# Reordering a split-precision input projection: high-part products two tiles ahead, the last chunks' splits earlier, the decode rows' transposes one block later

## The chip, the cores and the metric

The kernel runs on one NeuronCore of one Trainium2 chip. The metric is device time in microseconds from the start to the end of the program. Besides the plain timed runs there is one profiled execution; its trace gives the start and end of every instruction on the five engines: TensorE (PE; its weight loads are PEld), VectorE (DVE), ScalarE (ACT), GpSimd (POOL) and SyncE (SP), which here issues nearly all DMA copies (SPq is its queue).

## The reference

One inference step of a hybrid decoder layer for two request groups: a prompt of 512 tokens and 8 decode rows of one token each, model width 1024, float32.

```python
def mix_input(x, pos, g_norm_mix, w_in, g_q, g_k):
    xn = rms_norm(x, g_norm_mix)
    z = xn @ w_in                                  # (1024 x 3072)
    q, k, v, b_gate, c_gate, u_in = jnp.split(z, SPLITS, axis=-1)   # 768,768,768,256,256,256
    q = rope(rms_norm(heads(q), g_q), pos)
    k = rope(rms_norm(heads(k), g_k), pos)
    return q, k, heads(v), b_gate, c_gate * u_in
# attention: 12 heads x 64, dilated causal windows (128,1), (512,4), (2048,16), merged by their denominators;
#   the decode rows read a cache of 1024 earlier keys and values
# short convolution over c_gate * u_in, gated by b_gate; both parts normed, then w_out (1024 x 1024)
# h = x + mix;  y = h + HierMoE(rms_norm(h)): 32 experts of width 256, two per token
```

The outputs are y for both groups, the keys and values of the prompt and of the decode rows, and the convolution's last rows.

## The kernel before

The program has stages that follow one another: norm and transpose of x; the input projection (to about 222 us); attention of the prompt by 24 pairs of heads; output projection and routing; 16 pairs of experts, whose weights are streamed; the sum of the results. The change lies in the input projection.

**Split precision.** w_in is loaded in 8 chunks of 384 columns (`wchunk`). Each chunk is split into a rounded copy `w_high` (ScalarE, `high(c, i)`, four pieces of a chunk) and the rest `w_low` = w - w_high (VectorE, `low(c, i)`, four pieces, written over the loaded chunk). x has been split in the same way into `xT_high` and `xT_low`. A product then has three parts: x_high by w_high and x_low by w_high (16 matmuls, here called the high part) and x_high by w_low (8 matmuls, the low part).

**Chunks 0 to 5** (q, k, v) are computed token tile by token tile (4 tiles, `t`), a tile of a chunk being a unit `n = 4c + t` that accumulates in bank `n % 3`: high part (L671, L672), low part (L676). Between units TensorE does small work for the 8 decode rows: `partial_sums(c+1)` (L652, the decode rows times the unsplit next chunk, before `low` overwrites it), `combine(c)` (L603, adds its four parts), and `turn_rot` (L593, transposes of a rotated q or k tile, three units behind; it waits until ScalarE has copied the transposes before out of bank 5, L1043).

**VectorE's norm and rotation**, `norm_rope`, runs once for each q or k unit and once for a chunk's decode rows: a sum of squares (L1302), then, after a root on ScalarE (L1049), a reciprocal (L1304), products (L1225), half of them on GpSimd (L1763), and a sum. The pieces `low(c+1, i)` of the next chunk are done between these. All of L1225 is one helper, `tt`.

**Decode scores.** `sample_scores(b)` on VectorE, b = 0 to 7, multiplies 1 row of q, copied to all partitions (`spread_q`, a DMA issued by SyncE), by the cached keys, and sums by head (L1225, L1327). SyncE issues key, q, value and chunk copies in one fixed order, and each waits for a score step or a chunk to be done. The scores are transposed by TensorE (`turn_scores`, L616, L618), VectorE and ScalarE form the softmax, `turn_probs` (L626, L628) transposes the probabilities, VectorE places them, and `sample_values(0)` and `sample_values(1)` (L640) multiply them by the cached value rows of sequences 0 to 3 and 4 to 7. The second four use the buffers of the first: SyncE loads them once `sample_values(0)` is done (`v_used`).

**Chunks 6 and 7** (B, C, u) are computed as 6 blocks `i` of 128 columns by all 512 tokens, high part L724 and L725, low part L729, with the decode steps in between. After the 6 blocks come `sample_values(1)`, `own_values` and the pairs of heads. SyncE loads w_out when block 5 is done, behind the last value rows in its queue.

Each engine works through its own list in order; semaphores join them.

Of the kernel before, what the change touches and what calls it, by code (L numbers as in the profile page):

```python
# [26 lines left out]
P = 128  # L27
SEQ, DEC, D = 512, 8, 1024
NT = SEQ // P
# [91 lines left out]
def build(nc, x_prompt, x_sample, cache_k, cache_v, state_conv, g_norm_mix, w_in, g_q, g_k, w_conv, g_attn_out,  # L121
# [3 lines left out]
    with ctx:  # L125
# [436 lines left out]
        def _(pe):  # L562
# [92 lines left out]

            partial_sums(0)
            pend = []
            for c in range(QKV_CHUNKS):
                pe.wait_ge(S["w_high_done"], 4 * (c + 1))
                for t in range(NT):  # L660
                    n = unit(c, t)

                    if 3 <= n < QK_CHUNKS * NT + 3:
                        pe.wait_ge(S["z_copied"], n - 2)
                    elif n >= 3:
                        pe.wait_ge(S["v_evac"], n - 2 - QK_CHUNKS * NT)
                    cols = slice(t * P, (t + 1) * P)
                    if c == 0:
                        pe.wait_ge(S["x_evac"] if t < 2 else S["x_evac_p"], 2 * (t % 2) + 2)
                    for k in range(KD):  # L670
                        pe.matmul(bank[n % 3][:, 0:CW], xT_high[:, k, cols], w_high[c][:, k, :], start=(k == 0), stop=False)  # L671
                        pe.matmul(bank[n % 3][:, 0:CW], xT_low[:, k, cols], w_high[c][:, k, :], start=False, stop=False)  # L672
                    if t == 0:
                        pe.wait_ge(S["w_low_done"], 4 * (c + 1))
                    for k in range(KD):
                        last = pe.matmul(bank[n % 3][:, 0:CW], xT_high[:, k, cols], w_low[c][:, k, :],  # L676
                                         start=False, stop=(k == KD - 1))
                    last.then_inc(S["z_done"], 1)
                    if (c, t) == (0, 0):
                        turn_state()  # L680
                    if t == 0 and c <= 4 or (c, t) == (5, 2):
                        partial_sums(c + 1)
                    if t == 1:
                        combine(c)
                    if c < QK_CHUNKS:
                        pend.append((c, t))
                    if len(pend) > 3 or (c >= QK_CHUNKS and pend):
                        turn_rot(*pend.pop(0))
# [25 lines left out]
            for i in range(6):  # L714
# [16 lines left out]
                if i == 0:  # L731
                    combine(6)
                    turn_scores()
# [1161 lines left out]
```

## Time and profile before

| | us |
|---|---|
| median of 3 runs (674.38, 675.0, 678.39) | 675.0 |
| the profiled execution's own time | 671.45 |
| its span, first to last instruction | 669.8 |
| TensorE busy in the span | 545.2 (81%) |
| VectorE busy | 286.7 (43%) |
| ScalarE busy | 149.5 (22%) |
| GpSimd busy | 104.3 (16%) |

The mean granted clock of TensorE is 0.92 of 2.4 GHz. The page's slices show two stretches in which the DMA engines are almost wholly busy, in the experts' stage, and the input projection as a stretch in which TensorE and VectorE are both busy. A share of busy time is a mean over stages, so the rows below are taken from the projection alone. Times in the timelines are us from the start of the span; a row gives start, length, engine, line, operation, output and inputs, partitions and shape, the count, and in brackets the idle time of the engine before it with what ended it.

### The profile page before, as it was taken

Reading aid. Unit: us, or ns where it says so; the run is one execution under the profiler, and the core shown is the slowest. Engines: PE = TensorE matmul, PEld = TensorE weight load, DVE = VectorE, ACT = ScalarE, POOL = GpSimd, SP = SyncE. Lnnn points to the kernel's source line nnn. Section 1 sums busy time; section 2 is a strip of 40 time slices with the busy share of each in tenths; the row PEclk is TensorE's granted clock in tenths of the full one; section 3 lists DMA queues with packets and bytes.
Section 4 is the critical chain, followed back from the end, with each engine's and each line's share of the span. In section 5 each row is a group of like instructions: output and inputs, shape, how many; then the busy total and the mean of one; then the engine's idle time right before and its main releaser. Section 6 shows DMA issues by size and latency. Waiting matters only on the chain.

```text
span 669.8 us, 7971 instructions
## 1 busy us (share of the span) xinstructions
PE 545.2 (81%) x2798; PEld 323.0 (48%) x2798; DVE 286.7 (43%) x647; ACT 149.5 (22%) x351; POOL 104.3 (16%) x141
## 2 busy tenths in 40 slices
PE   3698889898599999899999516899996869797930
PEld 3486788797376588763555412333332323233300
DVE  4866776876521578732467440211211111111107
ACT  5433343323121356730000100210110000000000
POOL 0333454400000000000002232112212110201000
PEclk9998999999699999979999756999999898989975
DMA  7942323177906900029601901899999999999819
GB/s 267 292 129 93 97 72 139 35 248 243 304 0 187 375 7 1 1 83 426 279 31 54 386 1 55 365 421 420 420 420 420 421 420 421 420 422 419 335 50 353
DMA packets 42931, 159.66 MB, mean 238 GB/s; under 512 B 9048, under 2 KB 18208, under 8 KB 30584
## 3 DMA queue, kind: packets, MB, share of 16 engines
q1 hardware_dynamic: 36816, 146.95, 57.1%
q0 software_dynamic: 6080, 12.26, 4.9%
q8 instruction: 20, 0.33, 0.2%
q14 instruction: 15, 0.12, 0.1%
HBM read 151.56 MB, written 16.05 MB: 250 GB/s over the span
## 4 chain that ended last, share of the span: by engine, by line
PE 38%; SPq 21%; DVE 14%; DMA 10%; issue 8%; ACT 5%; POOL 3%; POOLq 0%; DVEq 0%; ACTq 0%
SPq L486 11%; PE bank L935 6%; SPq L500 6%; PE bank L890 4%; PE bank L960 4%; PE bank L791 3%; SPq L495 3%; DMA x<-q_rows 3%; POOL ring L1763 3%; DMA ring<-in_w_down_dram 3%; DVE work L1225 2%; PE bank L702 2%; PE bank L776 2%; DVE split L1225 2%; PE bank L676 2%
## 5 line engine op out<-in xcount | busy, mean ns | idle before, releaser
L935 PE MATMUL bank<-ring,work 128*64 128x512 f32 x512 | 121.7, 631 | 21.8 <-DMA ring<-in_w_up_dram 20.4
L935 PEld LDWEIGHTS bank<-ring,work 128*64 128x64 f32 x512 | 39.8, 145 | 102.1 <-issue 84.7
L671 PE MATMUL bank<-split 128*128 128x384 f32 x192 | 66.8, 348 | 0.0
L960 PE MATMUL bank<-ring,work 128*64 128x512 f32 x256 | 60.2, 613 | 7.6 <-ACT work L1198 7.6
L1225 DVE TENSOR_TENSOR work<-work,bank 128x256 f32<-128x256 f32 x16 | 6.7, 421 | 138.4 <-ACT work L1194 138.4
L672 PE MATMUL bank<-split 128*128 128x384 f32 x192 | 64.7, 337 | 0.0
L1763 POOL TENSOR_TENSOR ring<-ring 128x192 f32<-128x192 f32 (+1 forms) x40 | 38.0, 967 | 48.9 <-DVEq L1313 48.9
L890 PE MATMUL bank<-ring 128*128 128x512 f32 x96 | 42.6, 595 | 0.0
L676 PE MATMUL bank<-split 128*128 128x384 f32 x192 | 38.2, 340 | 4.5 <-DVE split L1225 4.5
L1225 DVE TENSOR_TENSOR split<-ring,split 128x768 fp32r<-128x768 f32 (+1 forms) x36 | 39.8, 1144 | 2.0 <-PE bank L652 1.6
L671 PEld LDWEIGHTS bank<-split 128*128 128x128 f32 x192 | 36.4, 190 | 3.8 <-issue 1.3
L1793 POOL DMA_DIRECT2D hn_rows<-work x5 | 2.8, 564 | 223.4 <-DVE work L1589 223.4
L960 PEld LDWEIGHTS bank<-ring,work 128*64 128x64 f32 x256 | 17.3, 139 | 40.1 <-issue 28.7
L676 PEld LDWEIGHTS bank<-split 128*128 128x128 f32 x192 | 33.6, 189 | 6.1 <-DVE split L1225 6.1
L672 PEld LDWEIGHTS bank<-split 128*128 128x128 f32 x192 | 36.5, 190 | 0.0
L1147 ACT ACTIVATE ring<-ring,st 128x512 f32<-128x512 f32 (+3 forms) x48 | 26.6, 554 | 42.5 <-DVE st L1397 42.5
L1667 DVE COPY work<-bank 128x512 f32<-128x512 f32 x16 | 11.1, 692 | 57.8 <-PE bank L960 57.8
L1194 ACT ACTIVATE work<-bank 128x256 f32<-128x256 f32 x16 | 6.1, 384 | 122.7 <-PE bank L935 122.6
L1225 DVE TENSOR_TENSOR work<-bank,gain_f 128x512 f32<-128x512 f32 (+1 forms) x42 | 26.0, 660 | 16.0 <-issue 14.0
L944 PE MATMUL bank<-ident,work 128*128 128x128 f32 x128 | 18.4, 289 | 16.6 <-DMA work<-hn_rows,pay_sb 16.6
L791 PE MATMUL bank<-ring 128*128 128x64 f32 x240 | 29.9, 271 | 0.4 <-DVE ring L1225 0.3
L791 PEld LDWEIGHTS bank<-ring 128*128 128x128 f32 x240 | 28.7, 192 | 0.9 <-DVE ring L1225 0.8
(214 smaller groups left out, 762.3 us busy)
## 6 DMA issues: line engine op xcount, KB each, us to landing
ring<-in_w_down_dram SPq DMA_DIRECT2D x32, 1024.0 KB, 27.3
ring<-in_w_gate_dram SPq DMA_DIRECT2D x30, 1024.0 KB, 19.8
ring<-in_w_up_dram SPq DMA_DIRECT2D x30, 1024.0 KB, 22.8
ring<-in_w_in_dram SPq DMA_DIRECT2D x8, 1536.0 KB, 9.6
x<-in_x_prompt_dram SPq DMA_DIRECT2D x8, 512.0 KB, 7.9
ring<-in_w_out_dram SPq DMA_DIRECT2D x1, 4096.0 KB, 13.1
ring<-results SPq DMA_DIRECT2D x4, 1024.0 KB, 7.8
x<-q_rows SPq DMA_DIRECT2D x8, 384.0 KB, 6.4
```

Of the source, the lines that this page charges most:

```text
L486: sp.dma_start(gate_up[s][h][:, o, :, :], w[0, ds(e, 1)].rearrange("e (p k) f -> p (e k) f", p=P)).then_inc(gu_in[s], 16)
L500: sp.dma_start(down[s][h], w_down[0, ds(e, 1)].rearrange("e (p k) n -> p (e k) n", p=P)).then_inc(dn_in[s], 16)
L671: pe.matmul(bank[n % 3][:, 0:CW], xT_high[:, k, cols], w_high[c][:, k, :], start=(k == 0), stop=False)
L672: pe.matmul(bank[n % 3][:, 0:CW], xT_low[:, k, cols], w_high[c][:, k, :], start=False, stop=False)
L676: last = pe.matmul(bank[n % 3][:, 0:CW], xT_high[:, k, cols], w_low[c][:, k, :], start=False, stop=(k == KD - 1))
L791: last = pe.matmul(bank[6 + u % 2][:, h * DH:(h + 1) * DH], probs_t[u % 2][h][:, j * P:(j + 1) * P], v_rows[:, j, (2 * hp + h) * DH:(2 * h ...
L890: last = pe.matmul(bank[g][:, :], src, wout[:, k, cols], start=(k == rng[0]), stop=(k == rng[-1]))
L935: last = pe.matmul(bank[2][64 * h:64 * h + 64, :], xgT[:, k, 64 * h:64 * h + 64], gate_up[s][h][:, :, k, :], start=(k == 0), stop=(k == KD ...
L960: last = pe.matmul(bank[4 + j][64 * h:64 * h + 64, :], hT[:, c, 64 * h:64 * h + 64], down[s][h][:, c, j * 512:(j + 1) * 512], start=(c == ...
L1147: act.activation(buf, buf, ACT.Exp, bias=nmax[:, u % 4:u % 4 + 1], scale=-1.0, accum_out=den[:, u % 24:u % 24 + 1]).then_inc(S["exp_done"], 1)
L1225: return dve.tensor_tensor(out, a, b, op)
L1763: last = pool.tensor_tensor(sv[:, :, a * half:(a + 1) * half], zv[:, :, b * half:(b + 1) * half], bc(rope_g[2 * (cc // 2) + 1][0:w, t, a * ...
```

## The change

In chunks 0 to 5 the high parts of tiles 0 and 1 are computed one after the other, then the low part of tile 0, and, behind the small work that stood there, the low part of tile 1. Tiles 2 and 3 are as before. The wait for `w_low` stands before the first low part.

Chunk 6's split moves: on ScalarE two high pieces behind unit (5, 1) and two behind (5, 2), instead of one each behind (5, 1) and (5, 2), and two behind (5, 3); on VectorE two low pieces each behind `sample_scores(5)` and `sample_scores(6)`, instead of three behind `sample_scores(7)` and one behind the decode rows' own scores. Chunk 7's low pieces move ahead of the placing of the probabilities; its high pieces ahead of the softmax's exponential on ScalarE.

On TensorE `turn_scores` moves from behind block 0 to behind block 1, `turn_probs` from block 1 to block 2, and `sample_values(0)` from block 3 to block 4.

```diff
             for c in range(QKV_CHUNKS):
                 pe.wait_ge(S["w_high_done"], 4 * (c + 1))
-                for t in range(NT):
...
+                by_high(c, 0)
+                by_high(c, 1)
+                if c == 0:
+                    turn_state()
+                by_low(c, 0)
+                if c <= 4:
+                    partial_sums(c + 1)
+                turn_next((c, 0) if c < QK_CHUNKS else None)
+                by_low(c, 1)
+                combine(c)
+                turn_next((c, 1) if c < QK_CHUNKS else None)
+                for t in (2, 3):
+                    by_high(c, t)
+                    by_low(c, t)
+                    if (c, t) == (5, 2):
+                        partial_sums(c + 1)
+                    turn_next((c, t) if c < QK_CHUNKS else None)
...
                 if i == 0:
                     combine(6)
+                if i == 1:
                     turn_scores()
-                if i == 1:
-                    turn_probs()
                     partial_sums(7)
                     turn_gates(0)
                 if i == 2:
                     pe.wait_ge(S["gates_read"], 1)
                     combine(7)
+                    turn_probs()
                 if i == 3:
                     turn_gates(1)
+                if i == 4:
                     sample_values(0)
-                if i == 4:
                     prompt_scores(0)
             sample_values(1)
...
-                    for i in ([(0, 1), (2, 3), (), ()], [(0, 1), (2, 3), (), ()], [(), (0,), (1,), (2,)])[max(c - 3, 0)][t]:
+                    for i in ([(0, 1), (2, 3), (), ()], [(0, 1), (2, 3), (), ()], [(), (0, 1), (2, 3), ()])[max(c - 3, 0)][t]:
                         high(c + 1, i)
...
-            high(6, 3)
             gate_copy(0)
             gate_row_copy(0)
-
-            act.wait_ge(S["soft_in"], 1)
-            act.activation(prob_s[0:96, :], neg_s[0:96, :], ACT.Exp, bias=nm_s[0:96, :], scale=-1.0,
-                           accum_out=den_s[0:96, :]).then_inc(S["soft_done"], 1)
             high(7, 0)
             high(7, 1)
             gate_copy(1)
             high(7, 2)
             high(7, 3)
+            act.wait_ge(S["soft_in"], 1)
+            act.activation(prob_s[0:96, :], neg_s[0:96, :], ACT.Exp, bias=nm_s[0:96, :], scale=-1.0,
+                           accum_out=den_s[0:96, :]).then_inc(S["soft_done"], 1)
...
             for b in range(2, DEC):
                 sample_scores(b)
-            for i in range(3):
-                low(6, i)
+                if b in (5, 6):
+                    for i in range(2):
+                        low(6, 2 * (b - 5) + i)
...
-            low(6, 3)
...
+            for i in range(4):
+                low(7, i)
             dve.wait_ge(S["probs_turned"], 1)
             dve.wait_ge(S["zero_rows"], 1)
...
-            for i in range(4):
-                low(7, i)
```

`by_high`, `by_low` and `turn_next` hold the old loop's lines: `by_high` the wait for the bank and the 16 matmuls (now L667, L668), `by_low` the wait for `w_low` if t is 0 and the 8 matmuls (now L677), `turn_next` the queue of transposes. The lines of the later parts shift by 19 to 21: block high parts are L745 and L746, their low part L750.

TensorE, units (0, 0) and (0, 1) and what stands between them (L609 transposes the convolution's state, L652 is the next chunk's sum for the decode rows, L603 combines), before:

```order
L672 MATMUL bank<-split 128x384
L676 MATMUL bank<-split 128x384 x8
L609 MATMUL bank<-ident,rt 128x16 x2
L652 MATMUL bank<-ring,work 32x384 x8
L671 MATMUL bank<-split 128x384
L672 MATMUL bank<-split 128x384
...
L676 MATMUL bank<-split 128x384 x8
L603 MATMUL bank<-work,small 8x384
```

and after, with both high parts ahead of the first row:

```order
L668 MATMUL bank<-split 128x384
L609 MATMUL bank<-ident,rt 128x16 x2
L677 MATMUL bank<-split 128x384 x8
L652 MATMUL bank<-ring,work 32x384 x8
L677 MATMUL bank<-split 128x384 x8
L603 MATMUL bank<-work,small 8x384
```

The 16 matmuls of the second high part went from behind L652 to ahead of the first low part.

TensorE, the ends of blocks 2 to 5 (L709, later L730, transposes gates, L640 is the product with cached values, L702, later L723, the first pair of scores), before:

```order
L603 MATMUL bank<-work,small 8x384
...
L729 MATMUL bank<-split 128x512 x8
L709 MATMUL bank<-ident,ring 128x8 x3
L640 MATMUL bank<-work,ring 32x384 x2
L640 MATMUL bank<-x,ring 32x384 x2
...
L729 MATMUL bank<-split 128x512 x8
L702 MATMUL bank<-ring 128x512 x2
...
L729 MATMUL bank<-split 128x512 x8
L640 MATMUL bank<-work,ring 32x384 x2
```

and after:

```order
L603 MATMUL bank<-work,small 8x384
L626 MATMUL bank<-ident,rt 128x96 x2
L628 MATMUL bank<-ident,st 8x96
...
L750 MATMUL bank<-split 128x512 x8
L730 MATMUL bank<-ident,ring 128x8 x3
...
L750 MATMUL bank<-split 128x512 x8
L640 MATMUL bank<-work,ring 32x384 x2
L640 MATMUL bank<-x,ring 32x384 x2
...
L723 MATMUL bank<-ring 128x512 x2
...
L750 MATMUL bank<-split 128x512 x8
L640 MATMUL bank<-work,ring 32x384 x2
```

The first product with cached values stands one block nearer to the second: block 5 and the pair of scores are between them, where blocks 4 and 5 and the scores were.

VectorE, score steps 5 to 7 (L1225 with L1327, later L1244 with L1346) and the low pieces of chunk 6 (split<-ring,split), before:

```order
L1225 TENSOR_TENSOR work<-work,x 128x1536
L1327 TENSOR_REDUCE rt<-work 128x2x12
L1225 TENSOR_TENSOR x<-x 128x1536
L1327 TENSOR_REDUCE rt<-x 128x2x12
L1225 TENSOR_TENSOR x<-x 128x1536
L1327 TENSOR_REDUCE rt<-x 128x2x12
L1225 TENSOR_TENSOR split<-ring,split 128x768 x3
L1225 TENSOR_TENSOR work<-work 8x768
L1358 TENSOR_REDUCE st<-work 8x12
L1225 TENSOR_TENSOR split<-ring,split 128x768
```

and after:

```order
L1244 TENSOR_TENSOR work<-work,x 128x1536
L1346 TENSOR_REDUCE rt<-work 128x2x12
L1244 TENSOR_TENSOR split<-ring,split 128x768 x2
L1244 TENSOR_TENSOR x<-x 128x1536
L1346 TENSOR_REDUCE rt<-x 128x2x12
L1244 TENSOR_TENSOR split<-ring,split 128x768 x2
L1244 TENSOR_TENSOR x<-x 128x1536
L1346 TENSOR_REDUCE rt<-x 128x2x12
L1244 TENSOR_TENSOR work<-work 8x768
L1378 TENSOR_REDUCE st<-work 8x12
```

The four low pieces went from behind step 7 and behind the decode rows' own scores to behind steps 5 and 6.

## Rows read from the trace of the kernel before

**Rows 1.** Waits of TensorE, 0 to 235 us: total us, times, longest us

```profile
PE bank L729 <- DVE split L1225: 7.2, 1, 7.2
...
PE bank L593 <- ACT ring L1043: 5.5, 3, 1.8
...
PE bank L676 <- DVE split L1225: 4.5, 5, 2.1
PE bank L724 <- ACT split L1017: 2.0, 1, 2.0
```

**Rows 2.** Timeline of VectorE: sums of squares that open the norm steps

```profile
34.18 0.56 DVE L1302 TENSOR_REDUCE st<-ring 128x6 f32<-128x384 f32 x1 [0.65 <-ACT ring L1047]
...
40.19 0.56 DVE L1302 TENSOR_REDUCE st<-ring 128x6 f32<-128x384 f32 x1 [2.02 <-ACT ring L1047]
...
54.42 0.54 DVE L1302 TENSOR_REDUCE st<-ring 128x6 f32<-128x384 f32 x1
...
59.37 0.55 DVE L1302 TENSOR_REDUCE st<-ring 128x6 f32<-128x384 f32 x1 [1.00 <-PE bank L593]
...
64.76 0.56 DVE L1302 TENSOR_REDUCE st<-ring 128x6 f32<-128x384 f32 x1 [1.40 <-PE bank L593]
...
73.80 0.53 DVE L1302 TENSOR_REDUCE st<-ring 128x6 f32<-128x384 f32 x1
```

**Rows 3.** Timeline of TensorE, chunks 0 to 2: low parts, row sums, transposes

```profile
31.84 1.68 PE L676 MATMUL bank<-split 128*128 128x384 f32 x8 [1.84 <-DVE split L1225]
...
33.68 1.50 PE L652 MATMUL bank<-ring,work 128*32 128x384 f32 x16
...
54.08 2.06 PE L676 MATMUL bank<-split 128*128 128x384 f32 x8 [2.13 <-DVE split L1225]
56.08 2.72 PE L652 MATMUL bank<-ring,work 128*32 128x384 f32 x16
...
75.19 0.52 PE L593 MATMUL bank<-ident,work 128*128 128x128 f32 x3 [1.84 <-ACT ring L1043]
```

**Rows 4.** Timeline of VectorE: score step 5, first low pieces of chunk 6

```profile
159.31 1.76 DVE L1225 TENSOR_TENSOR work<-work,x 128x1536 f32<-128x1536 f32 x1 [5.23 <-DMA x<-q_rows]
...
170.83 2.69 DVE L1225 TENSOR_TENSOR split<-ring,split 128x768 fp32r<-128x768 f32 x3
```

**Rows 5.** Timeline of TensorE, blocks 0 to 5 and the value products

```profile
176.27 3.78 PE L729 MATMUL bank<-split 128*128 128x512 f32 x8 [7.16 <-DVE split L1225]
179.98 1.45 PE L603 MATMUL bank<-work,small 128*8 128x384 f32 x2
...
193.39 1.98 PE L729 MATMUL bank<-split 128*128 128x512 f32 x8
195.30 0.81 PE L603 MATMUL bank<-work,small 128*8 128x384 f32 x2
...
201.99 0.52 PE L640 MATMUL bank<-work,ring 128*32 128x384 f32 x2
...
204.71 0.50 PE L724 MATMUL bank<-split 128*128 128x512 f32 x1
...
210.37 1.13 PE L702 MATMUL bank<-ring 64*128 64x512 f32 x4
...
218.75 0.52 PE L640 MATMUL bank<-work,ring 128*32 128x384 f32 x2 [1.57 <-DMA x<-in_cache_v_dram]
```

**Rows 6.** Windows: busy us (count) by engine; last: PEclk, DMA share, GB/s

```profile
55.20:58.60 3.40, 3.40 (x20) 1.03 (x18) 1.86 (x4) 0.97 (x3) 1.46 (x2) 0.50 0.02 6
164.40:167.80 3.40, 3.40 (x10) 2.66 (x9) 2.31 (x3) 0.00 (x0) 0.00 (x0) 0.50 0.84 252
...
206.00:217.50 11.50, 11.18 (x48) 8.08 (x46) 2.28 (x6) 1.52 (x4) 0.00 (x0) 1.00 0.97 266
```

**Rows 7.** Chain of waits, in order of time: start us, us, what

```profile
149.22 10.00 DMA x<-q_rows
...
204.84 0.36 SPq L411
```

More of the change, by code:

```diff
@@ L654, in partial_sums, with by_high, by_low, turn_next @@
                 last.then_inc(S["part_done"], 1)
+            def by_high(c, t):
+                n = unit(c, t)
+                if 3 <= n < QK_CHUNKS * NT + 3:
+                    pe.wait_ge(S["z_copied"], n - 2)
+                elif n >= 3:
+                    pe.wait_ge(S["v_evac"], n - 2 - QK_CHUNKS * NT)
+                cols = slice(t * P, (t + 1) * P)
+                if c == 0:
+                    pe.wait_ge(S["x_evac"] if t < 2 else S["x_evac_p"], 2 * (t % 2) + 2)
+                for k in range(KD):
+                    pe.matmul(bank[n % 3][:, 0:CW], xT_high[:, k, cols], w_high[c][:, k, :], start=(k == 0), stop=False)
+                    pe.matmul(bank[n % 3][:, 0:CW], xT_low[:, k, cols], w_high[c][:, k, :], start=False, stop=False)
+            def by_low(c, t):
+                n = unit(c, t)
+                cols = slice(t * P, (t + 1) * P)
+                if t == 0:
+                    pe.wait_ge(S["w_low_done"], 4 * (c + 1))
+                for k in range(KD):
+                    last = pe.matmul(bank[n % 3][:, 0:CW], xT_high[:, k, cols], w_low[c][:, k, :],
+                                     start=False, stop=(k == KD - 1))
+                last.then_inc(S["z_done"], 1)
+            def turn_next(unit_done=None):
+                if unit_done:
+                    pend.append(unit_done)
+                if len(pend) > 3 or (not unit_done and pend):
+                    turn_rot(*pend.pop(0))
             partial_sums(0)
@@ L659, in _ @@
                 pe.wait_ge(S["w_high_done"], 4 * (c + 1))
-                for t in range(NT):
[L661 to L681, printed above, removed]
-                        partial_sums(c + 1)
[L683 to L688, printed above, removed]
+                by_high(c, 0)
+                by_high(c, 1)
+                if c == 0:
+                    turn_state()
[10 more added lines that the diff above has]
+                    if (c, t) == (5, 2):
+                        partial_sums(c + 1)
+                    turn_next((c, t) if c < QK_CHUNKS else None)
             def prompt_scores(p):
```

## Prediction

> **What bounds the kernel now.** I read the page's busy shares first, then the waits of TensorE, then the timelines of TensorE and VectorE up to 235 us, then the chain of waits there, then the windows of granted clock and DMA. The change touches only the input projection (to about 222 us). Nothing behind it runs to a clock of its own: every later load or store is released by work that follows the projection, so whatever TensorE gains or loses at the second value product (218.75 us before) I carry one to one to the end. The question is how much earlier that product starts, and at which clock TensorE runs then.
>
> TensorE waits four ways in this part that matter here [rows 1]: 7.2 us once for the low part of chunk 6, 5.5 us in three waits of transposes for ScalarE, 4.5 us in five waits for a chunk's low part, and 2.0 us for chunk 6's high part; a fifth, of 1.57 us, is for value rows of the cache [rows 5]. In the first chunks the reader is to see VectorE: its norm-and-rotate steps stand nearly back to back, and only three of the steps up to 64.76 us wait for TensorE or for what hangs on it (2.02, 1.00 and 1.40 us) [rows 2]. The transposes at 75.19 us start 1.39 us after the VectorE step at 73.80 [rows 2, 3]: ScalarE's copy of the previous transposes stands behind the root for which that step delivers the sum. So VectorE and TensorE form one loop, and TensorE's own stalls are only partly the limit.
>
> **Part 1, high parts of two tiles ahead.** Nothing is added or removed: 16+16+8+8 matmuls instead of twice 16+8. The second tile's high part (about 2.8 us) now stands where TensorE waited for the low part. For chunk 0 the wait of 1.84 us is covered, chunk 1's of 2.13, and of the other three 0.5 in all [rows 1, 3]. The price: tile 0's result comes a high part later. For VectorE that means: chunk 0 tile 0 finishes about 0.9 us later, its step moves from 34.18 to 35.1, and VectorE is free for tile 1 at 39.1, where before it began at 40.19 after waiting [rows 2]. From there I set VectorE's steps back to back with their old spacing: 40.19 to 54.42 is 14.2, so tile 3 at 53.3; then 3.9 to chunk 1 tile 0 (57.2; before 59.37) and 3.9 to tile 1 (61.1; before 64.76). TensorE has delivered both by then (54.5 and 57.8 by its own row of work). Gain 3.6, call it 3.5.
>
> Where does that stall go? To the transposes behind chunk 1 tile 3. TensorE reaches them at about 67.7, but they still need VectorE's step of tile 2 plus 1.39 us: 75.19 - 3.5 = 71.6. The wait grows from 1.84 to about 3.9 us. That matters through the clock. After the wait of 2.13 us the low part took 2.06 and the next row sum 2.72, where the same groups take 1.55 and 1.50 in other places (the row sum at 33.68 is one) [rows 3]: 1.7 us lost, and the windows show 1.2 GHz (0.50) there [rows 6]. After 1.84 us nothing was lost. For 3.9 us I take 1.7; the bounds are 0 and 2.4 (below). From chunk 2 on each loop keeps only its short wait for the low part and the break around it, 0.3 us each; twice before the end of chunk 3, once in chunk 4. Lead at the end of chunk 3: 3.5 - 1.7 + 0.6 = 2.4 us for VectorE, 2.7 us for TensorE in chunk 4.
>
> **Part 2, chunk 6's split moved ahead.** On VectorE the four low pieces (0.9 us each, three in 2.69) stood behind all eight score steps; now two stand ahead of score step 6 and two ahead of step 7. Score step 5 is tied to its q copy, which landed at 159.31 after a wait of 5.23 [rows 4]; with the lead of 2.4 it ends at 160.4. Then 1.8 + 3.5 (step 6) + 1.8: the low part is ready at 167.5, against 176.27 [rows 4, 5]. Both high pieces on ScalarE move ahead too; the 2.0 us wait of block 0 for them goes [rows 1]. TensorE reaches the low part at about 162.6 and waits 4.9 us instead of 7.16. Queued behind VectorE's early pieces is score step 7, and behind that the scores' transposes; those now come a block later and are covered (VectorE done at about 173, TensorE there at 175). The cost of moving them is nothing; without that cover it would be step 7's 3.5 us and more.
>
> **Part 3, the decode rows' steps one block later.** From the low part of block 0 to the end of block 3 TensorE has the same work in another order: 176.27 to 201.99 is 25.7 us. Of these 2.4 were clock: 3.78 against 1.98 for the low part, 1.45 against 0.81 for the combination, after the idle 7.16 [rows 5]. I take 2.0 for 4.9 us idle, so 25.3. Low part of chunk 7: now ahead of the placing of the probabilities, hidden under block 2. Block 3 is done at 167.5 + 25.3 = 192.8, 9.2 us ahead.
>
> But the first value product (sample_values(0)) goes from behind block 3 to behind block 4. Block 4 takes 5.7 us (204.71 to 210.37), the product 2.7: it ends at 201.2, against 204.71, a lead of 3.5 [rows 5]. Its end frees the buffers of the last four sequences' value rows: SyncE then issues twelve copies, the first at 204.84 [rows 7], and the second product started at 218.75, 14.0 us after the first. That time is DMA: the queues are 0.97 busy from 206 to 217.5 at 266 GB/s, 3.1 MB [rows 6]. Before, TensorE had two blocks and one pair of scores (12.5 us) to put over these 14.0, and waited 1.57. Now it has one block and the scores, 6.8 us, and waits 7.2. The second product starts at 201.2 + 14.0 = 215.2, a lead of 3.5.
>
> **What the clock takes back.** The products, own values, scores and transposes behind this wait are all in the chain of waits, piece after piece on TensorE. After 7.16 us idle the loss was 2.4; before, after 1.57, none. Net lead 3.5 - 2.4 = 1.1 us.
>
> **Sum.** 671.45 (time of the profiled execution) - 1.1 = 670.3. The median of the runs is 675.0, so I forecast 675.0 - 1.1 = 673.9: a large wait removed, another of the same size made, no difference that can be measured.
>
> **A rule weighed.** After block 5 SyncE issues the 4 MB load of w_out, now at 208.0, with 6.0 us of value rows still to move (to 217.5 - 3.5 = 214.0); before they had just ended. Does it slow them? The q copy of score step 5, 0.4 MB behind a chunk and key rows, took 10.0 us [rows 7]; it was issued last, so this shows waiting behind earlier bytes and says little about later ones. Taking it as the nearest I charge 0. If the two share the engines evenly, 6.0 becomes 12.0. The Trainium skill (DMA: Bandwidth & Descriptors, section Queues, rings and completion order) says that an engine takes turns between queue rows, but takes the descriptors of one row's ring in order; by it w_out, on the same row, costs nothing here, and the sum stays. No row of this case separates the two.
>
> **Rivals.**
> - The value rows are not what the second product must wait for, or land after some 7 us. For it: all twelve copies are issued in some 6 us; against it: the busy window [rows 6]. The second product then starts at 208.0, a lead of 10.7 with no clock loss: 664.3. Chance 0.05.
> - The clock holds at 2.4 GHz through the new waits. Then 1.7 + 2.0 + 2.4 come on top: lead 7.2, 667.8. For it: three waits of 1.8 us cost nothing; against it: behind both waits of 2.0 and 2.13 us the windows show 0.50 [rows 6]. Chance 0.12.
> - The first chunks bring nothing, because VectorE's loop with ScalarE and GpSimd sets their pace and TensorE's longer wait costs the clock twice: lead -2.5 + 1.1 = -1.4, 676.4. Chance 0.15.
> - Slower, one mechanism: w_out's load shares the engines with the value rows. +6.0, 673.9 + 6.0 = 679.9. It decides the sign once it costs over 1.1 us, and over 7.9 it would be more than 1%. Chance 0.08.
> - The forecast: waits exchanged, 671 to 676, chance 0.60.
>
> **How the numbers follow.** 1% (6.75 us) is about what a measurement of this kernel can tell from no change. Faster by more: the first rival and half of the second, 0.11. Slower by more: half of the w_out rival and a little for waits that I don't see, 0.06. Between: 0.83. The range for 8 in 10 reaches to the second rival and near the fourth: 667.5 to 678.5.
>
> **What would show it.** In the changed profile: no wait for the low part in chunk 0 and under 0.5 us in chunk 1; a transposes' wait of 3 to 4 us behind chunk 1 tile 3; the wait for chunk 6's low part 4 to 6 us, ending near 167.5; first value product ending near 201; a wait for value rows of 7 us, followed by half clock. Wrong if the second value product starts before 212 or after 218, or if the granted clock stays at 1.00 behind it.

## The result, and the profile after

The changed kernel takes 677.15 us in the median of 20 runs, the kernel before 674.04 in 20 runs beside it: ratio 1.0046, 95% interval 1.0023 to 1.0068. I had forecast 1.1 us less; it is 3.1 us more. The time lies inside the range, and a change under 1% was the case with most of the chance, but the sign is wrong and the interval excludes no change.

The waits of TensorE in the projection, as in [rows 1]:

```profile
PE bank L593 <- ACT ring L1064: 9.7, 3, 3.6
PE bank L640 <- DMA x<-in_cache_v_dram: 8.6, 1, 8.6
PE bank L750 <- DVE split L1244: 5.5, 1, 5.5
```

The five waits for a chunk's low part (L676 before) and the wait for chunk 6's high part are gone. The three waits of transposes grew from 5.5 to 9.7 us, and the value rows' wait from 1.57 to 8.6.

VectorE's steps, sums of squares, as in [rows 2]: chunk 1 tile 1 and 3, then chunk 2 tile 0 and 1, chunk 3 tile 0 and 2.

```profile
60.72 0.55 DVE L1321 TENSOR_REDUCE st<-ring 128x6 f32<-128x384 f32 x1
...
74.92 0.54 DVE L1321 TENSOR_REDUCE st<-ring 128x6 f32<-128x384 f32 x1
...
82.13 0.56 DVE L1321 TENSOR_REDUCE st<-ring 128x6 f32<-128x384 f32 x1 [3.24 <-PE bank L593]
...
86.02 0.55 DVE L1321 TENSOR_REDUCE st<-ring 128x6 f32<-128x384 f32 x1
...
108.57 0.56 DVE L1321 TENSOR_REDUCE st<-ring 128x6 f32<-128x384 f32 x1 [4.13 <-PE bank L593]
...
121.47 0.53 DVE L1321 TENSOR_REDUCE st<-ring 128x6 f32<-128x384 f32 x1
```

To chunk 1 tile 1 it went as forecast: 60.72 against 64.76 in [rows 2], a lead of 4.0. Then VectorE's step of tile 0 waits for TensorE's transposes (L593), 3.24 us in chunk 2 and 4.13 in chunk 3. Neither wait was in my sum. Part of each is TensorE's lower clock in the high parts just before: with the clock at 2.4 GHz (run warm below) they are 1.67 and 1.47 us.

TensorE's timeline, as in [rows 3] and [rows 5]: the transposes behind tile 3 of chunks 1, 2 and 3, the first low part of chunk 3, and the later places.

```profile
71.10 0.52 PE L593 MATMUL bank<-ident,work 128*128 128x128 f32 x3 [3.57 <-ACT ring L1064]
...
96.43 0.87 PE L593 MATMUL bank<-ident,ring 128*128 128x128 f32 x3 [3.08 <-ACT ring L1064]
...
105.02 1.55 PE L677 MATMUL bank<-split 128*128 128x384 f32 x8
...
107.93 0.55 PE L593 MATMUL bank<-ident,work 128*128 128x128 f32 x3
...
122.87 0.87 PE L593 MATMUL bank<-ident,work 128*128 128x128 f32 x3 [3.08 <-ACT ring L1064]
...
174.01 3.63 PE L750 MATMUL bank<-split 128*128 128x512 f32 x8 [5.46 <-DVE split L1244]
...
204.44 0.52 PE L640 MATMUL bank<-work,ring 128*32 128x384 f32 x2
...
207.16 1.13 PE L723 MATMUL bank<-ring 64*128 64x512 f32 x4
...
222.53 0.85 PE L640 MATMUL bank<-work,ring 128*32 128x384 f32 x2 [8.58 <-DMA x<-in_cache_v_dram]
```

The transposes behind tile 3 start at 71.10, 4.1 us ahead of before (75.19), then at 96.43 and at 122.87. The loop from one to the next takes 25.3 and 26.4 us. In the kernel before, the same transposes came at 75.19, 98.15 and 121.14: 23.0 each. So the lead of 4.1 us has become a lag of 1.7 by chunk 4. The windows, columns as in [rows 6], show the granted clock: in chunk 3 behind its wait, later in chunk 4 when it is full again, and behind the second value product's start:

```profile
98.00:101.00 3.00, 3.00 (x11) 3.00 (x11) 2.79 (x4) 0.18 (x1) 1.42 (x2) 0.50 1.05 393
128.00:131.00 3.00, 3.00 (x20) 3.00 (x19) 1.84 (x4) 0.00 (x0) 1.52 (x3) 1.00 0.20 71
...
222.50:227.50 5.00, 4.97 (x32) 1.58 (x32) 0.00 (x0) 0.00 (x0) 0.00 (x0) 0.50 1.02 408
```

The two profiled executions differ by 9.3 us in span (679.1 and 669.8), the medians by 3.1. The profiled execution of the changed kernel, 680.72 us, is the slowest of its 20. Of the 9.3 us, 3.8 are the later second product, 2.9 the half clock behind it, and 2.6 lie behind the start of the next pair of scores, where the two programs are the same: from there to the end the kernel before took 446.9 us and the changed kernel 449.5, and the other twelve profiles 448.2 to 449.4. So the verdicts go by the timed runs, and the profiles say where time goes, each for one execution.

### The profile page after: what moved, and what is told of

Its sections match the earlier page's. It is cut to its first block, busy times and chain, and to the rows that moved or that the text cites. A ratio compares the mean times of both kernels' runs of the same rounds, so it can differ in the third digit from the quotient of the medians.

```text
span 679.1 us, 7971 instructions
## 1 busy us (share of the span) xinstructions
PE 550.9 (81%) x2798; PEld 328.7 (48%) x2798; DVE 286.5 (42%) x647; ACT 148.9 (22%) x351; POOL 104.2 (15%) x141
## 4 chain that ended last, share of the span: by engine, by line
PE 39%; SPq 21%; DVE 12%; DMA 11%; issue 6%; ACT 5%; POOL 4%; POOLq 0%; DVEq 0%; ACTq 0%
SPq L486 11%; PE bank L956 6%; SPq L500 6%; PE bank L911 4%; POOL ring L1782 4%; PE bank L981 3%; DMA x<-q_rows 3%; PE bank L812 3%; SPq L495 3%; DMA ring<-in_w_down_dram 3%; DVE work L1244 2%; PE bank L723 2%; PE bank L797 2%; DVE rt L1244 2%; DVE ring L1244 2%
## 5 line engine op out<-in xcount | busy, mean ns | idle before, releaser
L667 PE MATMUL bank<-split 128*128 128x384 f32 x192 | 69.7, 363 | 0.0
L668 PE MATMUL bank<-split 128*128 128x384 f32 x192 | 67.7, 353 | 0.0
L1244 DVE TENSOR_TENSOR work<-work,bank 128x256 f32<-128x256 f32 x16 | 6.7, 421 | 138.6 <-ACT work L1213 138.6
L667 PEld LDWEIGHTS bank<-split 128*128 128x128 f32 x192 | 39.1, 203 | 3.4 <-issue 1.3
L1244 DVE TENSOR_TENSOR split<-ring,split 128x768 fp32r<-128x768 f32 (+1 forms) x36 | 39.8, 1143 | 1.1 <-PE bank L652 0.7
L668 PEld LDWEIGHTS bank<-split 128*128 128x128 f32 x192 | 38.9, 203 | 0.0
L677 PE MATMUL bank<-split 128*128 128x384 f32 x192 | 37.8, 339 | 0.1
L677 PEld LDWEIGHTS bank<-split 128*128 128x128 f32 x192 | 33.3, 188 | 1.1 <-issue 0.6
L1244 DVE TENSOR_TENSOR work<-bank,gain_f 128x512 f32<-128x512 f32 (+1 forms) x42 | 26.0, 660 | 16.1 <-PE bank L965 16.0
## 6 DMA issues: line engine op xcount, KB each, us to landing
ring<-in_w_down_dram SPq DMA_DIRECT2D x32, 1024.0 KB, 26.4
ring<-in_w_gate_dram SPq DMA_DIRECT2D x30, 1024.0 KB, 23.5
```

The lines of the kernel that those rows point to most:

```text
L1244: return dve.tensor_tensor(out, a, b, op)
```

## The experiments

**A table of all.** The changed kernel and twelve more, each as a ratio to the kernel before on the same chip. The medians of the kernel before were 674.0 to 674.6 us beside the first nine rows and 676.2 beside the last four, so ratios compare across these groups better than times.

| kernel | median us | ratio | 95% interval |
|---|---|---|---|
| changed kernel | 677.15 | 1.0046 | 1.0023 to 1.0068 |
| order_only | 675.64 | 1.002 | 0.9991 to 1.0049 |
| splits_only | 676.18 | 1.002 | 0.9998 to 1.0041 |
| values_back | 668.94 | 0.9921 | 0.9893 to 0.9949 |
| turn_first | 683.37 | 1.0123 | 1.0099 to 1.0147 |
| turn_mid | 675.02 | 1.0011 | 0.9977 to 1.0045 |
| warm | 673.76 | 0.9987 | 0.9959 to 1.0014 |
| warm_late | 674.43 | 0.9997 | 0.9972 to 1.0023 |
| hold_wout | 676.56 | 1.0022 | 0.9991 to 1.0052 |
| splits_back | 667.86 | 0.9885 | 0.9849 to 0.9921 |
| best_mid | 665.58 | 0.9852 | 0.9813 to 0.9891 |
| best_early | 666.54 | 0.9853 | 0.9817 to 0.9889 |
| best_fill | 662.02 | 0.9799 | 0.9763 to 0.9835 |

**The parts alone.** order_only puts only the new chunk order into the kernel before; splits_only is the changed kernel with the old chunk loop.

```diff
 # order_only, against the kernel before
-                for t in range(NT):
...
+                by_high(c, 0)
+                by_high(c, 1)
...
+                by_low(c, 0)
...
+                by_low(c, 1)
...
 # splits_only, against the changed kernel: the same edit the other way
```

> The kernel before with the new order of chunks 0 to 5 on TensorE alone (high parts of tiles 0 and 1 ahead); splits, decode steps and value products stay as before. Theory A (VectorE's step for tile 0 waits for the transposes of three units back, which now stand behind the second high part; the loop gets longer, TensorE's wait behind tile 3 stays at 3 us and the clock falls in each chunk): slower than before by 1.5 to 4 us, ratio 1.002 to 1.006; waits of VectorE for transposes of 3 to 4 us in chunks 2 and 3, granted clock 0.5 behind each tile 3. Theory B (the loss of the whole change lies in the value rows and the clock behind them; the chunk order gains what was forecast): faster by 2 to 4 us, ratio 0.994 to 0.997.

> The changed kernel with the old order of chunks 0 to 5; chunk 6's and 7's splits moved, decode steps one block later. Theory A: the chunk order made the loss, so this one stands at the kernel before: -2 to +1 us, ratio 0.997 to 1.002; wait for value rows 7 to 9 us. Theory B: the loss lies here, +4 to +6 us, ratio 1.006 to 1.009.

Measured: 1.002 (0.9991 to 1.0049) and 1.002 (0.9998 to 1.0041). Each alone is at or a little above no change; their medians stand 1.0 and 1.6 us above that of before. Together that is about what the change costs, but both intervals include no change, so such a sum is not shown. Both ratios lie at the edge that theory A named (1.002), and the waits are those of theory A. Theory B for order_only, a gain of 2 to 4 us, falls: its interval ends at 0.9991. Theory B for splits_only, 4 to 6 us, falls too. TensorE's waits in order_only:

```profile
71.00 0.56 PE L593 MATMUL bank<-ident,work 128*128 128x128 f32 x3 [3.57 <-ACT ring L1064]
...
96.32 0.87 PE L593 MATMUL bank<-ident,ring 128*128 128x128 f32 x3 [3.08 <-ACT ring L1064]
122.72 0.87 PE L593 MATMUL bank<-ident,work 128*128 128x128 f32 x3 [3.08 <-ACT ring L1064]
...
222.33 0.52 PE L640 MATMUL bank<-work,ring 128*32 128x384 f32 x2 [1.45 <-DMA x<-in_cache_v_dram]
```

and in splits_only:

```profile
75.03 0.52 PE L593 MATMUL bank<-ident,work 128*128 128x128 f32 x3 [1.83 <-ACT ring L1043]
...
120.97 0.52 PE L593 MATMUL bank<-ident,work 128*128 128x128 f32 x3 [1.84 <-ACT ring L1043]
...
170.91 3.78 PE L729 MATMUL bank<-split 128*128 128x512 f32 x8 [5.23 <-DVE split L1223]
...
219.16 0.85 PE L640 MATMUL bank<-work,ring 128*32 128x384 f32 x2 [8.07 <-DMA x<-in_cache_v_dram]
```

The first has the changed kernel's loops (25.3 and 26.4 us) and the old value rows' wait; the second the old loops and the new wait of 8 us. In it block 0's low part starts 5.4 us earlier than in [rows 5], and the second value product 0.4 us later, at half the clock: the exchange of waits that I had forecast. In size it is less exact: my terms without the lead of the chunks (203.6 for the first product's end, 14.0 to the second) give 217.6, and it is 219.16.

**The value product.**

```diff
 # values_back, against the changed kernel
                 if i == 3:
                     turn_gates(1)
-                if i == 4:
                     sample_values(0)
+                if i == 4:
                     prompt_scores(0)
```

> The changed kernel with the first value product behind block 3 again, as in the kernel before; all else changed. Both theories: the value rows' copies start a block (5.7 us) earlier; the wait for them falls from 8.6 us to 1.5 to 3 and the clock stays up behind it. Gain against the changed kernel 6 to 9 us: -3 to -6 us against before, ratio 0.991 to 0.996. If the rows' wait is hidden by something else, or their copies take longer when started earlier, the gain is under 3 us.

Measured: 0.9921, 668.94 us, 8.2 us under the changed kernel. The second product starts at

```profile
213.59 0.52 PE L640 MATMUL bank<-work,ring 128*32 128x384 f32 x2 [1.45 <-DMA x<-in_cache_v_dram]
```

with a wait of 1.45 us and groups of 0.52 us, not 0.85. The gain lies in the expected 6 to 9 us. One moved step was worth 1.2%; it is the largest single term that I moved, and it went the wrong way: a block of 5.7 us ahead of the step that releases the copies, and the half clock (2.9 us) behind the longer wait.

**Where the transposes stand.** VectorE writes rotated tiles into three buffers in turn, `rot[n % 3]`; its step for unit n waits until unit n - 3 is transposed. In the old loop the transposes of unit 4c - 3 stood 6.5 us behind those after tile 3 (75.19 to 81.70 in chunk 2). In the changed loop a second high part stands between.

```diff
 # turn_first, against the changed kernel
                 by_high(c, 0)
+                turn_next((c, 0) if c < QK_CHUNKS else None)
                 by_high(c, 1)
...
-                turn_next((c, 0) if c < QK_CHUNKS else None)
 # turn_mid, against the changed kernel
                 by_high(c, 1)
                 if c == 0:
                     turn_state()
+                turn_next((c, 0) if c < QK_CHUNKS else None)
                 by_low(c, 0)
...
-                turn_next((c, 0) if c < QK_CHUNKS else None)
```

> The changed kernel with one edit: the transposes of the unit three back stand between the high parts of tile 0 and tile 1, not behind the low part. All else changed, the value product too. Theory A: VectorE's waits of 3 to 4 us for these transposes go, the loop of chunks 2 and 3 falls from 26.4 us to 22 to 24; gain against the changed kernel 3 to 7 us, so -4 to 0 us against before, ratio 0.994 to 1.000. Theory B: no difference to the changed kernel, ratio 1.003 to 1.006.

> The changed kernel with one edit: the transposes of the unit three back stand between tile 1's high part and tile 0's low part (behind the low part and the row sum in the changed kernel; between the two high parts in turn_first, where they waited for ScalarE's copy of the transposes before). The value product stays behind block 4. Theory A (the rotation buffers, freed by these transposes, hold VectorE up in chunks 2 and 3): VectorE's waits of 3.2 and 4.1 us shrink to under 1.5, TensorE's waits behind tile 3 of chunks 2 and 3 from 3.08 to about 1.5, loop of chunk 3 from 26.4 to 22.4-23.5 us; gain against the changed kernel 3 to 5 us, ratio to before 0.997 to 1.001. Theory B (the loop is set by ScalarE's root and copy, whatever TensorE's order): no gain, 1.003 to 1.006.

turn_first measured 1.0123, the opposite of what I expected. TensorE's waits in it:

```profile
54.50 0.61 PE L593 MATMUL bank<-ident,work 128*128 128x128 f32 x3 [4.74 <-ACT ring L1064]
...
75.73 0.52 PE L593 MATMUL bank<-ident,work 128*128 128x128 f32 x3 [2.05 <-ACT ring L1064]
80.95 0.52 PE L593 MATMUL bank<-ident,ring 128*128 128x128 f32 x3 [1.92 <-ACT ring L1064]
```

So early, the transposes must wait for ScalarE's copy of those before, which stands behind the root of chunk c - 1 tile 3, and that behind VectorE's step: 4.74 us in chunk 1, then mostly two waits a chunk instead of one. VectorE's wait for the transposes is gone, but TensorE now waits for them, tile 0 comes later still, and VectorE waits up to 4.4 us for ScalarE's square of it. turn_mid, one high part later, is the place between the two:

```profile
72.13 0.52 PE L593 MATMUL bank<-ident,work 128*128 128x128 f32 x3 [2.03 <-ACT ring L1064]
...
96.47 0.52 PE L593 MATMUL bank<-ident,ring 128*128 128x128 f32 x3 [2.02 <-ACT ring L1064]
120.84 0.52 PE L593 MATMUL bank<-ident,work 128*128 128x128 f32 x3 [2.02 <-ACT ring L1064]
```

The waits behind tile 3 fall from 3.08 to 2.02 us, the loops to 24.3 and 24.4. I expected 22.4 to 23.5. VectorE no longer waits for the transposes, but 2.25 and 2.08 us for ScalarE's square of tile 0, which comes when tile 0 is done. I expected under 1.5. Most of the difference is the clock, which fell behind each wait of 2.02 us. A window behind the second, and the start of tile 0's low part:

```profile
97.50:100.70 3.20, 3.20 (x12) 3.20 (x11) 3.20 (x4) 0.00 (x0) 1.61 (x3) 0.50 1.07 397
...
104.24 1.66 PE L677 MATMUL bank<-split 128*128 128x384 f32 x8
```

The same low part in hold_wout, where the clock held in this place and the transposes behind tile 3 start at 96.21:

```profile
102.14 1.55 PE L677 MATMUL bank<-split 128*128 128x384 f32 x8
```

From those transposes to the low part TensorE took 7.77 us in turn_mid, 0.24 of it for the transposes moved in between, and 5.93 in hold_wout. So the clock cost 1.6 us, and my estimate for turn_mid's loop without it is 24.3 - 1.6 = 22.7 us: below the changed order's 23.8 at full clock and the old order's 23.0. The buffer was what lengthened the loop. The time, 1.0011 (0.9977 to 1.0045), is 2.1 us under the changed kernel in the median, but the intervals overlap; the same edit is clear of noise beside values_back (best_mid, below).

**The clock.** 12 matmuls that nothing reads behind tile 3 of chunks 1 to 3 (warm), and 40 in the wait for the last value rows (warm_late):

```diff
 # warm, against the changed kernel
+                    if t == 3 and 1 <= c <= 3:
+                        for k in range(12):
+                            pe.matmul(bank[6][:, 0:CW], xT_high[:, k % KD, 0:P], xT_high[:, k % KD, 0:CW],
+                                      start=True, stop=True)
                     turn_next((c, t) if c < QK_CHUNKS else None)
 # warm_late, against the changed kernel
+            for k in range(40):
+                pe.matmul(bank[5][:, 0:CW], xT_high[:, k % KD, 0:P], xT_high[:, k % KD, 0:CW], start=True, stop=True)
             sample_values(1)
```

> The changed kernel with 12 matmuls of 384 columns into an unused bank (2.1 us; nothing reads them) behind tile 3 of chunks 1 to 3, where TensorE waits 3.1 to 3.6 us. Clock theory (the wait lets the clock fall to 1.2 GHz and that costs 1.9 to 2.7 us a chunk): granted clock 1.00 behind tile 3, the loop of chunk 3 falls from 26.4 to about 23.8 us, chunk 4 starts 5 to 7 us earlier, the time falls by 3 to 6 us. Rival (the clock costs nothing because VectorE is the limit): the loop stays at 25 to 26.4 us, the time within 1.5 us of the changed kernel.

> The changed kernel with 40 matmuls of 384 columns into bank 5 (7.0 us; nothing reads them) in the wait for the last value rows, 8.6 us long. Clock theory: the second value product and what follows run at 2.4 GHz, 0.52 us a group where it was 0.85; gain 2 to 3 us against the changed kernel, ratio 1.000 to 1.003; the product's start does not move. Rival (what follows is bound by VectorE and ScalarE): gain under 1 us.

Both bear the clock theory out. warm: 0.9987, its interval apart from the changed kernel's, 3.4 us less. Its transposes behind tile 3:

```profile
71.45 0.52 PE L593 MATMUL bank<-ident,work 128*128 128x128 f32 x3 [1.51 <-ACT ring L1068]
...
95.20 0.52 PE L593 MATMUL bank<-ident,ring 128*128 128x128 f32 x3 [0.99 <-ACT ring L1068]
118.99 0.52 PE L593 MATMUL bank<-ident,work 128*128 128x128 f32 x3 [1.01 <-ACT ring L1068]
```

Loops of 23.75 and 23.79 us, where the changed kernel took 25.3 and 26.4. Chunk 4 starts 3.9 us earlier; I had expected 5 to 7. VectorE's waits for the buffer, chunks 2 and 3:

```profile
80.91 0.55 DVE L1325 TENSOR_REDUCE st<-ring 128x6 f32<-128x384 f32 x1 [1.67 <-PE bank L593]
...
104.68 0.56 DVE L1325 TENSOR_REDUCE st<-ring 128x6 f32<-128x384 f32 x1 [1.47 <-PE bank L593]
```

In the kernel before, VectorE waited for the buffer at tile 1 of these chunks:

```profile
87.73 0.56 DVE L1302 TENSOR_REDUCE st<-ring 128x6 f32<-128x384 f32 x1 [0.86 <-PE bank L593]
...
110.72 0.55 DVE L1302 TENSOR_REDUCE st<-ring 128x6 f32<-128x384 f32 x1 [0.65 <-PE bank L593]
```

That is 0.8 us less each time, which is the difference of the loops at full clock (23.8 and 23.0). warm_late: 0.9997, 2.7 us less than the changed kernel; the second product's groups take 0.52 us again. Its interval and the changed kernel's just touch.

```profile
220.26 0.52 PE L640 MATMUL bank<-work,ring 128*32 128x384 f32 x2 [2.04 <-DMA x<-in_cache_v_dram]
```

**w_out behind the value rows.**

```diff
 # hold_wout, against the changed kernel
-            sp.dma_start(wout, w_out_v).then_inc(S["wout_in"], 16)
             sp.wait_ge(S["v_used"], 2)
+            sp.dma_start(wout, w_out_v).then_inc(S["wout_in"], 16)
```

> The changed kernel with the 4 MB load of w_out issued only when both value products are done, not behind block 5. If w_out's load took bandwidth from the value rows: from the end of the first product to the second 14.0 us, as in the kernel before, and not 15.4; gain up to 1.4 us, unless w_out then comes too late, which it should not (it is used some 60 us later). If not: 15.4 us as in the changed kernel.

The first product ends at 205.51 and the second starts at 219.54: 14.0 us, as before the change. In the six profiles where w_out is issued within 1.6 us of the last value copy it was 14.5 to 16.3 us (14.5 in turn_mid, 15.4 in the changed kernel, 16.3 in warm), 15.4 in the mean. In the eight where w_out comes 6.5 us behind that copy or later it was 13.5 to 15.1 (13.9 in order_only, 15.1 in best_early), 14.2 in the mean. The two ranges overlap, so one profile proves little; the means are 1.2 us apart. The bytes say more. The windows from the first value copy to the second product, in the changed kernel:

```profile
207.30:214.00 6.70, 6.65 (x28) 4.58 (x28) 1.33 (x5) 1.52 (x4) 0.00 (x0) 1.00 0.82 242
214.00:222.50 8.50, 0.00 (x0) 0.00 (x1) 0.67 (x1) 0.00 (x0) 0.00 (x0) 0.75 1.03 281
```

and in hold_wout:

```profile
205.60:219.50 13.90, 6.71 (x28) 4.65 (x28) 2.00 (x5) 1.52 (x4) 0.00 (x0) 0.82 0.80 226
```

That is 4.0 MB in the changed kernel and 3.1 in hold_wout: about 0.9 MB of w_out moved before the last value rows landed. So the two loads do overlap, but the cost is about 1 us, not 6. The time, 0.6 us under the changed kernel, is within the noise. This run's trace gave something else:

```profile
96.21 0.52 PE L593 MATMUL bank<-ident,ring 128*128 128x128 f32 x3 [3.08 <-ACT ring L1064]
120.00 0.88 PE L593 MATMUL bank<-ident,work 128*128 128x128 f32 x3 [3.10 <-ACT ring L1064]
```

and its window behind the first of these, at 2.4 GHz throughout:

```profile
96.20:101.20 5.00, 4.99 (x30) 5.00 (x31) 4.49 (x7) 0.84 (x3) 2.77 (x3) 1.00 1.04 391
```

Same order of work, same wait of 3.08 us, and here the clock held: 23.8 us where the changed kernel's execution took 26.4, order_only's 26.4, values_back's 25.3 and warm_late's (untouched in this place) 25.1. A wait of this length costs from 0 to 2.6 us, by execution. The bare loop of the new order is 23.8, 0.8 us longer than the old 23.0.

**Putting together.** splits_back is values_back with the old chunk loop; best_mid is values_back with turn_mid's edit; best_early is values_back with the high parts ahead only in chunks 0 and 1; best_fill adds matmuls to best_early, 12 behind chunk 1's tile 3 and 20 between block 0's high and low part, which nothing reads.

```diff
 # best_early, against values_back
                 by_high(c, 0)
-                by_high(c, 1)
+                if c <= 1:
+                    by_high(c, 1)
...
+                if c > 1:
+                    by_high(c, 1)
                 by_low(c, 1)
 # best_fill, against best_early
+                    if (c, t) == (1, 3):
+                        fill(12)
...
+                if i == 0:
+                    fill(20)
```

> The old order in chunks 0 to 5, the splits and transposes of the change, first value product behind block 3: values_back without the chunk order. If the chunk order costs 1 to 2 us beside these: 667 to 668, ratio 0.988 to 0.991, faster than values_back by 1 to 2 us. If it gains: 0.994 or more.

> turn_mid and values_back together: transposes between tile 1's high part and tile 0's low part, first value product behind block 3. If the two gains add: 674.5 - 5.5 (values_back) - 2 (turn_mid against the changed kernel) = 666 to 668, ratio 0.988 to 0.992. If the chunk order has no part in the loss: 0.992 as values_back.

> values_back with the high parts of tiles 0 and 1 ahead only in chunks 0 and 1, where TensorE had waited 1.84 and 2.13 us; chunks 2 to 5 as in the kernel before. Theory A: the lead of 4 us at chunk 1's end stays (less 1.5 to 2 us of clock behind the wait of 3.6 us), the loops of chunks 2 and 3 are 23.0 us again with waits of 1.8 us at 2.4 GHz; chunk 4 starts 3 us earlier than in the kernel before: ratio 0.986 to 0.990. Theory B (order neutral): 0.992.

> best_early with 12 matmuls that nothing reads behind chunk 1's tile 3 (wait of 3.6 us) and 20 between block 0's high and low part (wait of 4 to 5 us). Clock theory: low part of block 0 in 2.0 and not 3.6 us, chunk 2's high parts at 2.4 GHz; 2 to 4 us less than best_early, ratio 0.982 to 0.987. Rival: within 1 us of best_early.

splits_back 0.9885, best_mid 0.9852, best_early 0.9853: all beat both kernels. splits_back stands 0.4% under values_back, so the chunk order seems to cost beside these too, though the intervals overlap. best_mid and best_early stand 0.7% under values_back, with intervals apart from its own (0.9813 to 0.9891 and 0.9817 to 0.9889 against 0.9893 to 0.9949). best_mid differs from it by the place of the transposes alone, so what that place does, to the buffer and to the waits and the clock behind it, shows in time and not only in traces. (The groups were timed on different chips, each against the kernel before there.) Against splits_back (0.9849 to 0.9921) the mended order may gain 0.3%, which is not shown. splits_back fell in its expected range; best_mid (expected 0.988 to 0.992) and best_early (0.986 to 0.990) came out faster than theirs. best_early's transposes behind tile 3 come at

```profile
70.65 0.88 PE L593 MATMUL bank<-ident,work 128*128 128x128 f32 x3 [3.60 <-ACT ring L1067]
...
94.65 0.52 PE L593 MATMUL bank<-ident,ring 128*128 128x128 f32 x3 [1.82 <-ACT ring L1067]
...
117.62 0.52 PE L593 MATMUL bank<-ident,work 128*128 128x128 f32 x3 [1.84 <-ACT ring L1067]
```

a lead of 3.5 us at chunk 4. best_fill, 662.02 us and 0.9799, is the best of all, 2% under the kernel before and better than I expected (0.982 to 0.987); its interval overlaps that of best_early. Its low part of block 0 waits little, because the added matmuls fill the wait, and runs at nearly full clock:

```profile
165.69 2.11 PE L762 MATMUL bank<-split 128*128 128x512 f32 x8 [1.28 <-DVE split L1256]
```

Of the 5.6 us by which its second product is earlier than best_early's in the profiles, 1.6 are a shorter time for the value rows (13.5 and 15.1 us), which the added matmuls do not explain.

## Why the prediction was wrong, point by point

**The lead by chunk 1.** Right. 3.5 to 3.6 us forecast, 4.0 measured at VectorE's step, 4.1 at the transposes; the stall moved behind chunk 1 tile 3 (3.57 us, forecast 3.9), and the low parts' waits went.

**"From chunk 2 on each loop keeps only its short wait for the low part."** Here the prediction fails. I took the price of the new order as "tile 0's result comes a high part later" and followed only the result. The transposes of unit 4c - 3 stand behind the same low part, and they free the buffer into which VectorE's step for tile 0 writes. That step waited 3.24 and 4.13 us, of which 1.67 and 1.47 remain at full clock (warm). I had each loop 0.3 us shorter than 23.0; it is 0.8 longer, shown by the loops at full clock (warm, hold_wout: 23.8). The list of what is queued behind the added work had one entry too few. My own rows held the hint: two of the three VectorE waits that I quoted, 1.00 and 1.40 us, name the transposes (L593) in [rows 2], and I read them as waits for a tile's result (a fourth wait in those rows, 0.65 us at 34.18, I passed over).

**The clock in the chunks.** The mechanism was right, its size and count were off. I charged 1.7 us once, behind chunk 1. Because the longer loop leaves waits of 3.1 us behind tile 3 of chunks 2 and 3 too, where there had been 1.8, the loss can come in every chunk: in the profiled execution about 1.5 us in chunk 2's loop and 2.6 in chunk 3's over the bare 23.8. Lead at the end of chunk 3 forecast 2.4, measured -1.7: 4.1 us off. Of these, 2.2 are the loops (0.8 longer instead of 0.3 shorter, twice), 2.4 the clock (4.1 lost, 1.7 charged), and the better start gives 0.5 back. My third rival (the first chunks bring nothing, the clock takes twice) is nearest to what happened, with the clock right, but its reason, VectorE's loop with ScalarE and GpSimd, was not the buffer.

**Chunk 6's split.** Right in kind: in splits_only, where no chunk order disturbs, the low part starts at 170.91 against 176.27, 5.4 us earlier, though score step 5 started 1.1 us later there (its q copy); I had 6.4 from the moving alone. In the changed kernel it starts at 174.01, forecast 167.5. Of these 6.5 us, 4.1 are the lost lead. Some 2 are the q copy of score step 5, for which VectorE waited 7.21 us, not 5.23. The wait for this copy differs from execution to execution (5.1 us in best_early, 7.6 in order_only, 7.9 in best_mid); why, I did not settle.

**From there to the value products.** Right: low part of block 0 to the end of block 3 took 24.8 us (25.3 forecast); the second product waits 8.6 us (7.2 forecast). The difference is the time from the first product to the second, 15.4 and not 14.0. About 1.2 us of that is w_out's load in the mean of the profiles, the rest their spread. I had charged 0 for it, on the strength of a row that could not show it. Some 0.9 MB of the load moved before the last value rows had landed, yet the 6 us of my fourth rival do not appear. The Trainium skill (DMA: Bandwidth & Descriptors, section Queues, rings and completion order) says that an engine takes the descriptors of one row's ring in order. The runs agree in so far as the cost stays near 1 us; that it is nothing, as I had by this rule, they do not bear out.

**The clock behind the value rows.** Right: from the second product to the next pair of scores took 7.04 us (222.53 to 229.57), against 4.1 before; 2.9 lost, 2.4 forecast, and warm_late wins 2.7 back in the median.

**The sum.** Forecast -1.1, measured +3.1. In the trace the second product starts 7.3 us later than forecast (222.53, not 215.2): 4.1 are the lead lost in the chunks, 2.4 the later score step and its copy, 1.3 the longer time for the value rows, and 0.5 came back in blocks 0 to 3. The largest term is the loop of chunks 2 and 3 with its clock. The timed runs agree: the medians miss the forecast by 4.2 us, and warm, which gives the chunks their clock back, measured 0.9987, 0.9 us under the kernel before and near the forecast, though its interval includes no change. The other terms vary more from execution to execution, and this profile is the slowest of 20: by its sizes alone no single term explains the sign. What I did not ask is whether the good parts could be kept: undoing one line's move gains 8.2 us. The prediction had this number, the 5.7 us of block 4, in its working.

## What to carry to other kernels

- When work is put ahead on an in-order engine, list everything queued behind it, not its product only: the small step that frees a buffer for another engine can be the one that is waited for. And where a step is moved earlier instead, ask what it waits for itself (turn_first).
- A step whose end starts a long transfer belongs as early as its inputs allow, even if it does little by itself.
- Where a change makes or lengthens a wait of TensorE on the critical path, read from the profile what the granted clock did behind waits of that size, and charge it once per occurrence (here 0 to 2.6 us for waits of 2.0 to 3.6 us); matmuls that nothing reads, put into the wait and shorter than it, can buy it back.

## What the runs showed of the hardware that I had not expected

- A wait of 3.08 us at the same place, with the same work around it, left the clock at 2.4 GHz in one execution and at 1.2 in others; the loop took 23.8, 25.1 or 26.4 us. Waits of 1.8 us behind tile 3 cost nothing in any profile. Waits of 2.04 and 2.13 us cost clock in the kernel before, and all three of 2.0 us behind tile 3 did in turn_mid, but 2.13 us in splits_back did not (below). So one profile does not tell what a wait of this size costs; several must be read. With 12 matmuls in the idle time the clock held, and the same loop took 23.75 and 23.79 us. The Trainium skill (TensorE: Matmul & The Clock Gate, section What's actually happening) says that activity releases a throttle which is otherwise on. The traces agree.
- A 4 MB load issued while about 1.5 MB of earlier copies of the same queue were still moving (an estimate: 3.1 MB less 242 GB/s for 6.7 us) delayed their landing by about 1 us: 14.5 to 16.3 us in six profiles, 13.5 to 15.1 in eight without it so close behind.

The wait of 2.13 us in splits_back, and the window behind it at full clock:

```profile
53.98 1.66 PE L676 MATMUL bank<-split 128*128 128x384 f32 x8 [2.13 <-DVE split L1223]
...
54.00:58.00 4.00, 4.00 (x31) 2.74 (x32) 2.44 (x6) 1.17 (x3) 1.47 (x2) 1.00 0.23 80
```
